# The last two feed-forwards of a four-layer kernel: up projections as seven block products, down projections spread between them

## The chip, the cores and the metric

The kernel runs on one core of a Trainium2 chip. The metric is the device time of one execution in microseconds, the median of several runs; lower is better. The profile is that of one more execution.

## The reference

A float32 transformer on 512 tokens of 1024 features: two blocks with convolutional feed-forwards, then two "hybrid" layers (differential attention, a gated recurrence, memory attention). What the change touches is the feed-forward of the two hybrid layers, here x is 512 x 1024, w_up 1024 x 5632, w_down 2816 x 1024:

```python
u = depthwise_conv_centred(x @ w_up, conv_w, conv_b)   # three taps over the tokens
gate, val = jnp.split(u, 2, axis=-1)
ffn = (jax.nn.silu(gate) * val) @ w_down
return layer_norm(DEEPNORM_ALPHA * x + ffn, ln2_g, ln2_b)
```

## The kernel before

Activations lie transposed, features on the partitions: X holds 8 tiles of 128 features x 512 tokens. A float32 product is made of three products of a shorter type: each operand is split in a high part and a low part (what the high part leaves), and PE adds high x high, high x low and low x high in one PSUM bank. HX holds both parts of the layer's input, FR those of the hidden activations.

**Weights.** They pass through a ring of SLOTS = 9 buffers of 128 x 1024. SyncE alone issues the loads, in one fixed order; the load of entry r waits until the user of entry r - 9 has freed it (L3516). A "unit" p is one weight tile. `cast_to` lets ScalarE (ACT) write its high part in WH[p % 3], after the load has landed and after PE has used unit p - 3; `rest_to` lets GpSimd (POOL) write the low part in WL[p % 3] and free the ring buffer (L452). Both take the units in order, and each engine runs its program in order, so a wait in it holds all that stands behind it. PE waits for the low part of each unit.

**Feed-forward before.** `ffn_plan` makes 44 up tiles (22 pairs of one gate and one val tile of 128 columns), 8 x 3 matmuls of 512 columns each. The hidden dimension is taken in two parts of 11 pairs; after each, 8 down groups (one for each output tile) run over its 11 hidden tiles, in two units of 6 and 5. For each up tile ACT makes the middle tap with the bias (L1051) and VectorE (DVE) the two outer taps from PSUM (L1055, L1058); then ACT makes silu (L1682), DVE gate x val (L1712), ACT the high part (L1688), DVE the low part (L1722). A down group is added to X by DVE (L2498, L2500); in the last part ACT squares X and POOL adds X and its square into the sums of the layer norm (L795).

**Start of a feed-forward.** The layer norm before it writes HX tile by tile (L896, L864). The first two up tiles run side by side behind it (`pair_pe`). `kept_a` (L904) then writes the normed X back, in the second layer with the casts of two units between. `mix_g` has left the low parts of units 0 to 2 ready.

## Time and profile before

| what | us |
|---|---|
| median of 3 runs (lowest, highest) | 3240.03 (3238.53, 3240.19) |
| span of the profiled execution | 3237.6 |
| PE busy | 3182.1 (98%) |
| first hybrid layer's feed-forward, up and down | about 2094 to 2446 |
| second one's | about 2874 to 3230 |

The span is the time from the first to the last instruction in the profile. The profile has no device time of its own execution; the span lies 2.4 us below the median of the runs. A matmul's duration in the profile holds its latency: the spacing of the starts says what one costs.

### The profile page before, as it was taken

The numbers are of one execution on the slowest core, as the hardware profiler recorded it, in microseconds if no ns is written. First come the engines' busy times: TensorE is split into PE (matmuls) and PEld (weight loads), VectorE is DVE, ScalarE is ACT, GpSimd is POOL, SyncE is SP. The second block draws the span as 40 slices with busy tenths as digits, with TensorE's granted clock in tenths as the row PEclk, the third lists the DMA queues.
The fourth block names the chain that finished last, engine by engine and source line by source line (L and its number), as shares of the span: only waits on it lengthen the run. The fifth ranks groups of instructions, "written<-read, shape, count | busy, mean of one in ns | idle before, by whom it ended". The sixth has DMA issues, their size and how long they took to land.

```text
span 3237.6 us, 40142 instructions
## 1 busy us (share of the span) xinstructions
PE 3182.1 (98%) x16204; PEld 2552.9 (79%) x16204; DVE 1591.0 (49%) x2605; ACT 1301.7 (40%) x2307; POOL 1329.3 (41%) x754
## 2 busy tenths in 40 slices
PE   7999999999999999999999999999999999999998
PEld 4876888888885557888886888888887788878886
DVE  5877366323337663423225685352432768455252
ACT  4322421312246774423334535342433544444243
POOL 2222423222254445444551234544455234454446
PEclk9999999999999999999999999999999999999999
DMA  7223334121132003233232111323223121222321
GB/s 274 105 96 121 124 110 147 49 66 66 52 115 103 20 8 116 93 93 105 82 117 72 54 59 53 117 93 101 96 90 114 46 70 45 62 98 76 116 79 55
DMA packets 85925, 288.17 MB, mean 89 GB/s; under 512 B 9803, under 2 KB 10379, under 8 KB 84972
## 3 DMA queue, kind: packets, MB, share of 16 engines
q1 hardware_dynamic: 85740, 285.60, 26.0%
q8 instruction: 128, 2.10, 0.3%
q14 instruction: 57, 0.47, 0.0%
HBM read 283.47 MB, written 2.10 MB: 88 GB/s over the span
## 4 chain that ended last, share of the span: by engine, by line
PE 89%; DVE 3%; issue 2%; POOL 2%; ACT 2%; DMA 1%; SPq 0%; POOLq 0%; DVEq 0%; ACTq 0%
PE ps L504 20%; PE ps L507 20%; PE ps L505 20%; PE ps L563 2%; PE ps L565 2%; PE ps L564 2%; PE ps L2153 2%; PE ps L3005 1%; PE ps L2596 1%; DMA ring<-in_w_mod 1%; PE ps L483 1%; PE ps L2223 1%; PE ps L478 1%; PE ps L522 1%; PE ps L2610 1%
## 5 line engine op out<-in xcount | busy, mean ns | idle before, releaser
L452 POOL TENSOR_TENSOR WL<-ring,WH 128x1024 fp32r<-128x1024 f32 (+2 forms) x427 | 926.6, 2173 | 1397.4 <-ACT WH L441 1397.0
L504 PE MATMUL ps<-HX,WH 128*128 128x512 f32 x1656 | 649.2, 392 | 0.0
L507 PE MATMUL ps<-HX,WL 128*128 128x512 f32 x1656 | 647.7, 391 | 0.0
L505 PE MATMUL ps<-HX,WH 128*128 128x512 f32 x1656 | 646.2, 390 | 0.0
L441 ACT CAST WH<-ring 128x1024 fp32r<-128x1024 f32 (+2 forms) x443 | 421.1, 951 | 529.5 <-PE ps L507 471.2
L504 PE MATMUL ps<-FR,WH 128*128 128x512 f32 x1120 | 418.8, 374 | 0.3
L505 PE MATMUL ps<-FR,WH 128*128 128x512 f32 x1120 | 409.7, 373 | 0.0
L507 PE MATMUL ps<-FR,WL 128*128 128x512 f32 x1120 | 389.4, 373 | 0.0
L504 PEld LDWEIGHTS ps<-HX,WH 128*128 128x128 f32 x1656 | 311.1, 188 | 67.2 <-issue 1.2
L507 PEld LDWEIGHTS ps<-HX,WL 128*128 128x128 f32 x1656 | 312.3, 189 | 45.0
L505 PEld LDWEIGHTS ps<-HX,WH 128*128 128x128 f32 x1656 | 311.3, 188 | 45.0
L1055 DVE SCALAR_TENSOR_TENSOR T<-ps,pv,T 128x511 f32<-128x511 f32 (+1 forms) x154 | 109.4, 711 | 346.5 <-ACT T L1051 342.3
L504 PEld LDWEIGHTS ps<-FR,WH 128*128 128x128 f32 x1120 | 210.3, 188 | 46.8 <-DVE FR L3218 1.1
L1051 ACT ACTIVATE T<-ps,pv 128x512 f32<-128x512 f32 (+1 forms) x154 | 112.7, 746 | 328.8 <-PE ps L507 317.3
L505 PEld LDWEIGHTS ps<-FR,WH 128*128 128x128 f32 x1120 | 210.4, 188 | 37.4
L507 PEld LDWEIGHTS ps<-FR,WL 128*128 128x128 f32 x1120 | 198.6, 189 | 29.9
L1010 DVE SCALAR_TENSOR_TENSOR X<-ps,mod,X 128x512 f32<-128x512 f32 x64 | 48.0, 751 | 301.1 <-PE ps L507 287.7
L1722 DVE TENSOR_TENSOR FR<-T,FR 128x512 fp32r<-128x512 f32 x110 | 138.8, 1277 | 62.7 <-ACT FR L1688 62.7
L505 PE MATMUL ps<-HC,WH 128*128 128x256 f32 x504 | 141.8, 281 | 0.0
L507 PE MATMUL ps<-HC,WL 128*128 128x256 f32 x504 | 141.5, 281 | 0.0
L504 PE MATMUL ps<-HC,WH 128*128 128x256 f32 x504 | 141.4, 281 | 0.0
L563 PE MATMUL ps<-WH,HX 128*128 128x512 f32 x320 | 126.8, 396 | 0.8 <-ACT AR L2694 0.8
(406 smaller groups left out, 5271.8 us busy)
## 6 DMA issues: line engine op xcount, KB each, us to landing
ring<-in_ffn_w_up SPq DMA_DIRECT2D x88, 512.0 KB, 3.2
ring<-in_w_up SPq DMA_DIRECT2D x88, 512.0 KB, 3.2
ring<-in_w_mod SPq DMA_DIRECT2D x64, 512.0 KB, 4.2
ring<-in_w_in_tok SPq DMA_DIRECT2D x40, 512.0 KB, 3.3
ring<-in_w_mod_columns SPq DMA_DIRECT2D x32, 512.0 KB, 4.1
ring<-in_w_in_feat SPq DMA_DIRECT2D x32, 512.0 KB, 3.2
ring<-in_ffn_w_down SPq DMA_DIRECT2D x32, 384.0 KB, 3.0
ring<-in_w_out SPq DMA_DIRECT2D x32, 384.0 KB, 3.1
```

The source lines that it names most:

```text
L441: act.copy(WH[:, p % SPLITS, 0:n], ring.ap(r)).then_inc(*split.a.up("high", p))
L452: pool.tensor_tensor(WL[:, p % SPLITS, 0:n], ring.ap(r), WH[:, p % SPLITS, 0:n], ALU.subtract).then_inc(*ring.frees(r, split.g, "low", p))
L504: pe.matmul(o, high, xh, first, False)
L505: pe.matmul(o, high, xl, False, False)
L507: m = pe.matmul(PS[bs[i]][:, 0:N], low, get(k)[0], False, last)
L563: pe.matmul(PS[bs[t]][:, :], xh[:, tt], high, k == 0, False)
L564: pe.matmul(PS[bs[t]][:, :], xh[:, tt], low, False, False)
L565: m = pe.matmul(PS[bs[t]][:, :], xl[:, tt], high, False, k == 7)
L1051: act.activation(dst, src, ACT.Identity, scale=w1, bias=b).then_inc(*steps.up("conv", *name))
L1055: dve.scalar_tensor_tensor(dst[:, 1:N], src[:, 0:N - 1], w0, dst[:, 1:N], ALU.mult, ALU.add).then_inc(*steps.up())
L1722: dve.tensor_tensor(lo, gate_tile(L, n, s, val_conv), hi, ALU.subtract).then_inc(*fw.v.up("low", L.name, n, s))
L2153: pe.matmul(PS[b][:, 0:c1 - c0], QT[n % 2][0:96, h, t * 128:t * 128 + 128], KT[n % 2][0:96, h, c0:c1], True, True).then_inc(*att.pe.up("sc ...
```

## The change

The two hybrid feed-forwards (L_ffb) get a plan and four engine programs of their own. Pairs 0 and 1 run as before. For the other 20 pairs the weights of a pair and the input are cut in 2 x 2 blocks (gate and val by the two halves of the 1024 features; tokens by halves of 256), and seven block products of 4 x 3 matmuls of 256 columns take the place of eight. The sums of weight blocks are made by DVE in the ring's buffers and in T, in float32; the sums of input blocks ("forms", XF) once for each layer, by DVE, then split by ACT and POOL. The products are summed in PSUM: each of them accumulates in a half of a bank, and copies by ACT (copy 1, 2, 3, 5) and two additions by DVE ("five right", "five both") put them where they are wanted. A pair takes four units: "11" (512 wide) in step i = j, "1 2" (1024) in the same step, "3 12" and "4 22" (1024 each) in step i = j + 1. The low part of "1 2" is made by DVE, the others by POOL. The hidden dimension is taken in parts of 3, 4, 5, 5 and 5 pairs, so that there are 40 down groups of one unit each; 28 of them stand one or two at a time behind the steps 4 to 21, one in step 22, 11 at the end. The ring has 8 buffers instead of 9, in the whole kernel.

```diff
-SLOTS = 9
+SLOTS = 8
-ARENA = 27200
+ARENA = 28224
+FRONT = 2
...
         HC = nc.alloc_sbuf_tensor_at("HC", [128, 8, 2, SC], F32R, offset=base + 4 * 20480)
+        XF = [nc.alloc_sbuf_tensor_at(f"XF{k}", [128, 2, 4, 256], F32R, offset=base + 4 * o)
...
+        def seven_plan(name, wname, dname, i):
+
+            L = Linear(ring, name)
+            L.sizes, L.nst, L.i, L.slots = [3, 4, 5, 5, 5], 1, i, 10
+            L.bounds = [sum(L.sizes[:p]) for p in range(len(L.sizes) + 1)]
+            up, down = dr[wname][i], dr[dname][i]
+            L.rows(up, 0, 2 * FRONT, 8, kind="up")
+            L.unit, L.downs, L.down_last = {}, {}, []
+            def made(kind, j, n, loads=()):
+                p = L.unit[kind, j] = len(ring.splits)
+                ring.splits.append((None, n))
+                ring.made[p] = (L, kind, j)
+                if loads:
+                    ring.carried[p] = [((L.name, x), up[x]) for j_ in loads for x in (2 * j_, 2 * j_ + 1)]
+
+            rows = [(x, n) for x in range(len(L.sizes)) for n in range(8)]
+
+            def some(at, n):
+                for _ in range(n):
+                    x, row = rows.pop(0)
+                    L.rows(down, row, row + 1, L.sizes[x], per=6, k0=L.bounds[x], kind=x)
+                    L.downs.setdefault(at, []).append(L.groups[-1])
+                    if row == 7:
+                        L.down_last.append(L.groups[-1].last)
+
+            after = dict(zip(range(4, 22), (2, 2, 2, 2, 2, 2, 2, 1, 1, 2, 2, 2, 1, 1, 1, 1, 1, 1)))
+            for j in range(FRONT, FT + 1):
+                if j < FT:
+                    made("11", j, 512, range(j, min(j + 2, FT)) if j == FRONT else range(j + 1, min(j + 2, FT)))
+                if j > FRONT:
+                    made("3 12", j - 1, 1024)
+                if j < FT:
+                    made("1 2", j, 1024)
+                else:
+                    some("between", 1)
+                if j > FRONT:
+                    made("4 22", j - 1, 1024)
+                some(j, after.get(j, 0))
+            some("end", len(rows))
             return L
...
+        in_vector |= {p for p, (_, kind, _) in ring.made.items() if kind == "1 2"}
+        def unit_source(p):
+
+            if p not in ring.made:
+                r = ring.place.get(p, 0)
+                return ring.ap(r), ring.landed(r)
+            L, kind, j = ring.made[p]
+            gate, val = raw_tiles(L, j)
+            if kind == "11":
+                return ring.ap(gate)[:, 0:512], ring.landed(gate)
+            if kind == "3 12":
+                return ring.ap(gate), sv.v.at("sum 3", L.name, j)
+            if kind == "1 2":
+                return T[:, 4:6, :].rearrange("p a b -> p (a b)"), sv.v.at("sum 2", L.name, j)
+            return ring.ap(val), sv.v.at("sum 4", L.name, j)
+
+        def low_up(steps, p):
+
+            if p not in ring.made:
+                return ring.frees(ring.place.get(p, 0), steps, "low", p)
+            up = steps.up("low", p)
+            L, kind, j = ring.made[p]
+            if kind == "4 22":
+                for r in raw_tiles(L, j):
+                    ring.frees_too(r, steps)
+            return up
...
         def cast_to(act, upto):
             while ring.cast <= min(upto, len(ring.splits) - 1):
                 p = ring.cast
                 ring.cast += 1
                 n = ring.splits[p][1]
-                r = ring.place.get(p, 0)
-                act.wait_ge(*ring.landed(r))
+                src, ready = unit_source(p)
+                act.wait_ge(*ready)
                 if p >= SPLITS:
                     act.wait_ge(*split.pe.at("used", p - SPLITS))
-                act.copy(WH[:, p % SPLITS, 0:n], ring.ap(r)).then_inc(*split.a.up("high", p))
+                act.copy(WH[:, p % SPLITS, 0:n], src).then_inc(*split.a.up("high", p))
...
+        def forms_v(dve, q):
+            for k in range(4):
+                dve.wait_ge(*nm.a.at("kept", q.name, k + 4))
+                b12, b21, b22 = BLOCKS[:, 2 * k + 1, :], BLOCKS[:, 2 * k + 8, :], BLOCKS[:, 2 * k + 9, :]
+                dve.tensor_tensor(raw_form(k, F1, 2).rearrange("p (a b) -> p a b", a=2), BLOCKS[:, 2 * k:2 * k + 10:9, :],
+                                  b12.unsqueeze(1).to_broadcast([128, 2, 256]), ALU.subtract).then_inc(*sv.v.up())
+                dve.wait_ge(*sv.v.now())
+                dve.scalar_tensor_tensor(raw_form(k, F2S), raw_form(k, F1), -1.0, b22, ALU.mult,
+                                         ALU.subtract).then_inc(*sv.v.up())
+                dve.wait_ge(*sv.v.now())
+                dve.scalar_tensor_tensor(raw_form(k, F4), raw_form(k, F2S), -1.0, b21, ALU.mult,
+                                         ALU.subtract).then_inc(*sv.v.up("forms", q.name, k))
+
+        def forms_a(act, q):
+            for k in range(4):
+                act.wait_ge(*sv.v.at("forms", q.name, k))
+                act.copy(XF[k][:, 0, :, :].rearrange("p a b -> p (a b)"), raw_form(k, 0, 4)).then_inc(
+                    *sv.a.up("forms", q.name, k))
+
+        def forms_g(pool, q):
+            for k in range(4):
+                pool.wait_ge(*sv.a.at("forms", q.name, k))
+                pool.tensor_tensor(XF[k][:, 1, :, :].rearrange("p a b -> p (a b)"), raw_form(k, 0, 4),
+                                   XF[k][:, 0, :, :].rearrange("p a b -> p (a b)"), ALU.subtract).then_inc(
+                    *sv.g.up("forms", q.name, k))
+
...
+        def product_pe(pe, p, at, out, x, ready=None, opens=None):
+
+            for k in range(4):
+                c = slice(at + k * 128, at + k * 128 + 128)
+                high, low = WH[:, p % SPLITS, c], WL[:, p % SPLITS, c]
+                xh, xl = x(k)
+                if ready is not None:
+                    for done in ready(k):
+                        pe.wait_ge(*done)
+                if k == 0 and opens == "whole bank":
+                    pe.matmul(out[0], high, HX[:, 0, 0, :], True, False)
+                else:
+                    pe.matmul(out[1], high, xh, k == 0 and opens == "half", False)
+                pe.matmul(out[1], high, xl, False, False)
+                m = pe.matmul(out[1], low, xh, False, k == 3)
+            return m
+
...
+            for i in range(FRONT, FT + 1):
+                j = i - 1
+                if i < FT:
+                    A[i], B[i] = bank.take_in("gate", "gate", name, i), bank.take_in("val", "val", name, i)
+                    C[i] = bank.take_in("five", "five", name, i)
+                    p = begin("11", i)
+                    if i < FRONT + 2:
+                        pe.wait_ge(*bank.free("val", name, i))
+                        pe.matmul(PS[B[i]][:, :], WH[:, p % SPLITS, 0:128], HX[:, 0, 0, :], True, True)
+                    pe.wait_ge(*bank.free("gate", name, i))
+                    product_pe(pe, p, 0, left(A[i]), block_of(0, 0), None, "whole bank").then_inc(*split.pe.up("used", p))
+                if j >= FRONT:
+                    p = begin("3 12", j)
+                    pe.wait_ge(*sv.a.at("copy 2", name, j))
+                    product_pe(pe, p, 0, right(B[j]), form_of(F3), formed).then_inc(*sv.pe.up("product 7", name, j))
+                    pe.wait_ge(*sv.v.at("five right", name, j))
+                    product_pe(pe, p, 512, left(A[j]), block_of(1, 0)).then_inc(*split.pe.up("used", p))
+                if i < FT:
+                    p = begin("1 2", i)
+                    pe.wait_ge(*bank.free("five", name, i))
+                    product_pe(pe, p, 0, left(C[i]), form_of(F1), formed, "half").then_inc(
+                        *sv.pe.up("product 5", name, i))
+                    pe.wait_ge(*sv.a.at("copy 1", name, i))
+                    product_pe(pe, p, 512, right(B[i]), form_of(F2S), formed).then_inc(*split.pe.up("used", p))
+                else:
+                    for g in L.downs["between"]:
+                        down(g)
+                if j >= FRONT:
+                    p = begin("4 22", j)
+                    product_pe(pe, p, 0, right(A[j]), block_of(1, 1)).then_inc(*sv.pe.up("product 3", name, j))
+                    pe.wait_ge(*sv.v.at("five both", name, j))
+                    product_pe(pe, p, 512, left(B[j]), form_of(F4), formed).then_inc(*split.pe.up("used", p))
+                for g in L.downs.get(i, ()):
+                    down(g)
+            for g in L.downs["end"]:
+                down(g)
+
...
+            forms_a(act, qf)
+            for g in [g for g in L.groups if g.key[0] == "up"]:
...
+            for i in range(FRONT, FT + 1):
+                j = i - 1
+                if FRONT < i < FT:
+                    cast_to(act, L.unit["11", i] + 3)
+                high(i - 2)
+                if i == FRONT:
+                    cast_to(act, L.unit["11", i] + 3)
+                if i < FT:
+                    act.wait_ge(*used("11", i))
+                    if i >= FRONT + 2:
+                        act.wait_ge(*bank.free("val", name, i))
+                    act.copy(val_bank(L, i)[:, 256:512], gate_bank(L, i)[:, 0:256]).then_inc(*sv.a.up("copy 1", name, i))
+                if j >= FRONT:
+                    act.wait_ge(*sv.pe.at("product 7", name, j))
+                    act.copy(val_bank(L, j)[:, 0:256], val_bank(L, j)[:, 256:512]).then_inc(*sv.a.up("copy 3", name, j))
+                    cast_to(act, L.unit["3 12", j] + 3)
+                if i < FT:
+                    act.wait_ge(*sv.pe.at("product 5", name, i))
+                    if i >= FRONT + 2:
+                        act.wait_ge(*sv.v.at("five both", name, i - 2))
+                    act.copy(five(i), ps("five", name, i)[:, 0:256]).then_inc(
+                        *bank.emptied(("five", name, i), sv.a, "copy 5", name, i))
+                    act.wait_ge(*used("1 2", i))
+                    act.copy(gate_bank(L, i)[:, 256:512], val_bank(L, i)[:, 256:512]).then_inc(
+                        *sv.a.up("copy 2", name, i))
+                    cast_to(act, L.unit["1 2", i] + 3)
...
+                if j >= FRONT:
+                    act.wait_ge(*sv.pe.at("product 3", name, j))
+                    act.wait_ge(*fw.v.at("low", name, j - 2, 0))
+                    conv_a(act, fw.a, (name, 2 * j, 0), T[:, j % 2, :], gate_bank(L, j)[:, :], cw(1, j), cb(j))
+                    cast_to(act, L.unit["4 22", j] + 3)
+                    act.wait_ge(*used("4 22", j))
+                    act.wait_ge(*sv.v.at("five both", name, j))
+                    conv_a(act, fw.a, (name, 2 * j + 1, 0), T[:, 2 + j % 2, :], val_bank(L, j)[:, :], cw(1, FT + j),
+                           cb(FT + j))
+                    act.wait_ge(*fw.v.at("conv", name, 2 * j, 0))
+                    act.activation(gate_bank(L, j)[:, :], T[:, j % 2, :], ACT.Silu).then_inc(
+                        *fw.a.up("silu", name, j, 0))
+                for g in L.downs.get(i, ()):
+                    down(g)
...
+            def sums_1_2(j):
+                gate, val = raw_tiles(L, j)
+                dve.wait_ge(*ring.landed(val))
+                dve.tensor_tensor(T[:, 4, :], ring.ap(val)[:, 0:512], ring.ap(val)[:, 512:1024], ALU.add).then_inc(
+                    *sv.v.up("sum 1", name, j))
+                dve.wait_ge(*ring.landed(gate))
+                dve.wait_ge(*sv.v.at("sum 1", name, j))
+                dve.tensor_tensor(T[:, 5, :], T[:, 4, :], ring.ap(gate)[:, 0:512], ALU.add).then_inc(
+                    *sv.v.up("sum 2", name, j))
+
+            def sums_3_4(j):
+                gate, val = raw_tiles(L, j)
+                dve.wait_ge(*low_done(L.unit["11", j]))
+                dve.tensor_tensor(ring.ap(gate)[:, 0:512], ring.ap(gate)[:, 0:512], ring.ap(val)[:, 0:512],
+                                  ALU.add).then_inc(*sv.v.up("sum 3", name, j))
+                dve.wait_ge(*sv.v.at("sum 3", name, j))
+                dve.tensor_tensor(ring.ap(val)[:, 0:512], T[:, 5, :], ring.ap(gate)[:, 512:1024],
+                                  ALU.add).then_inc(*sv.v.up("sum 4", name, j))
+
+            sums_1_2(FRONT)
+            forms_v(dve, qf)
...
+            for i in range(FRONT, FT + 1):
+                j = i - 1
+                if i < FT:
+                    rest_v(dve, L.unit["1 2", i])
+                low(i - 2)
+                if j >= FRONT:
+                    dve.wait_ge(*sv.a.at("copy 3", name, j))
+                    dve.wait_ge(*sv.a.at("copy 5", name, j))
+                    dve.tensor_tensor(val_bank(L, j)[:, 256:512], val_bank(L, j)[:, 256:512], five(j), ALU.add).then_inc(
+                        *sv.v.up("five both", name, j))
+                if i < FT:
+                    sums_3_4(i)
+                if i + 1 < FT:
+                    sums_1_2(i + 1)
+                if i < FT:
+                    dve.wait_ge(*sv.a.at("copy 2", name, i))
+                    dve.wait_ge(*sv.a.at("copy 5", name, i))
+                    dve.tensor_tensor(gate_bank(L, i)[:, 256:512], gate_bank(L, i)[:, 256:512], five(i),
+                                      ALU.add).then_inc(*sv.v.up("five right", name, i))
...
+                if j >= FRONT:
+                    taps(j, 0, gate_bank(L, j), None, T[:, j % 2, :])
+                    taps(j, 1, val_bank(L, j), ("val", name, j), T[:, 2 + j % 2, :])
+                    dve.wait_ge(*fw.v.now())
+                    dve.wait_ge(*fw.a.at("silu", name, j, 0))
+                    dve.scalar_tensor_tensor(gate_bank(L, j)[:, :], T[:, 2 + j % 2, :], -1.0, gate_bank(L, j)[:, :],
+                                             ALU.mult, ALU.mult).then_inc(*fw.v.up("gated", name, j, 0))
+                for g in L.downs.get(i, ()):
+                    down_v(dve, L, g)
+            low(FT - 1)
+            for g in L.downs["end"]:
+                down_v(dve, L, g)
+
+        def seven_g(pool, L, qf, q):
+            forms_g(pool, qf)
+            for g in L.downs["end"]:
+                rest_to(pool, g.last + 2)
+                if is_final(L, g):
+                    ln_sums_g(pool, q, g.key[1], lin.v.at("res", L.name, g.key, 0))
+            ln_g(pool, q)
+            rest_to(pool, g.last + 3)
...
-            ffn_v(dve, L_ffb[l], lambda j, n: col("conv_w_2", 132 * l + 44 * j + n), True, down)
+            seven_v(dve, L_ffb[l], lambda j, n: col("conv_w_2", 132 * l + 44 * j + n), ln_1[l], down)
...
-            last_ffn_a(act, L_ffb[l], ln_2[l], lambda j, n: col("conv_w_2", 132 * l + 44 * j + n),
-                       lambda n: col("conv_b_2", 44 * l + n), True)
+            seven_a(act, L_ffb[l], lambda j, n: col("conv_w_2", 132 * l + 44 * j + n),
+                    lambda n: col("conv_b_2", 44 * l + n), ln_1[l], ln_2[l])
...
-                ffn_pe(pe, L_ffb[l], lambda s: ready1)
+                seven_pe(pe, L_ffb[l], ln_1[l], ready1)
...
-                last_ffn_g(pool, L_ffb[l], ln_2[l])
+                seven_g(pool, L_ffb[l], ln_1[l], ln_2[l])
```

## Rows read from the trace of the kernel before

**Rows 1.** The page: span, PE's busy line, chain by engine.

```profile
span 3237.6 us, 40142 instructions
...
PE 89%; DVE 3%; issue 2%; POOL 2%; ACT 2%; DMA 1%; SPq 0%; POOLq 0%; DVEq 0%; ACTq 0%
```

**Rows 2.** Windows: window, length, busy us and count of PE, PEld, DVE, ACT, POOL; clock, DMA, GB/s.

```profile
2094.00:2446.00 352.00, 352.00 (x1578) 290.77 (x1577) 141.41 (x150) 133.72 (x175) 173.81 (x89) 1.00 0.30 97
2873.68:3230.00 356.32, 352.41 (x1581) 290.60 (x1579) 144.74 (x158) 137.59 (x184) 173.48 (x91) 1.00 0.25 80
```

**Rows 3.** Timeline of PE: start, duration; first matmuls of two neighbouring up tiles.

```profile
2873.68 0.39 PE L504 MATMUL ps<-HX,WH 128*128 128x512 f32 x1
...
2879.11 0.39 PE L504 MATMUL ps<-HX,WH 128*128 128x512 f32 x1
```

**Rows 4.** Timeline of PE in the first feed-forward: wide and narrow matmuls mixed.

```profile
599.95 0.39 PE L504 MATMUL ps<-HX,WH 128*128 128x512 f32 x1
...
602.51 0.28 PE L504 MATMUL ps<-HC,WH 128*128 128x256 f32 x1
602.63 0.28 PE L505 MATMUL ps<-HC,WH 128*128 128x256 f32 x1
602.75 0.40 PE L507 MATMUL ps<-HX,WL 128*128 128x512 f32 x1
...
611.53 0.40 PE L504 MATMUL ps<-HX,WH 128*128 128x512 f32 x1
```

**Rows 5.** Groups by form, 2094 to 2446, POOL: splitting a unit, layer-norm sums.

```profile
L452 POOL TENSOR_TENSOR WL<-ring,WH 128x1024 fp32r<-128x1024 f32 x43 | 103.2, 2401 | 128.5 <-ACT WH L441 128.5
L452 POOL TENSOR_TENSOR WL<-ring,WH 128x640 fp32r<-128x640 f32 x16 | 25.1, 1566 | 24.5 <-ACT WH L441 24.5
L795 POOL TENSOR_TENSOR T<-T,X 128x512 f32<-128x512 f32 x6 | 7.7, 1286 | 9.8 <-DVE X L2500 9.8
```

**Rows 6.** Timeline, start of the first hybrid feed-forward.

```profile
2087.91 5.03 ACT L904 ACTIVATE X<-X,pv 128x512 f32<-128x512 f32 x8
...
2095.14 0.39 PE L504 MATMUL ps<-HX,WH 128*128 128x512 f32 x1
```

**Rows 7.** Timeline of ACT, start of the second one.

```profile
2876.22 2.56 ACT L904 ACTIVATE X<-X,pv 128x512 f32<-128x512 f32 x4
```

**Rows 8.** Timeline of DVE and POOL: one DVE form beside a POOL operation, and alone.

```profile
2101.04 2.36 DVE L1712 TENSOR_TENSOR T<-T 128x512 f32<-128x512 f32 x1
...
2100.45 2.40 POOL L452 TENSOR_TENSOR WL<-ring,WH 128x1024 fp32r<-128x1024 f32 x1 [1.15 <-ACT WH L441]
...
2883.95 0.69 DVE L1712 TENSOR_TENSOR T<-T 128x512 f32<-128x512 f32 x1
```

**Rows 9.** Groups by form of the whole span: DVE subtraction of 1024, taps.

```profile
L1058 DVE SCALAR_TENSOR_TENSOR T<-ps,pv,T 128x511 f32<-128x511 f32 x132 | 99.0, 750 | 4.7
...
L429 DVE TENSOR_TENSOR WL<-ring,WH 128x1024 fp32r<-128x1024 f32 x12 | 16.5, 1377 | 1.6 <-ACT WH L441 1.6
```

**Rows 10.** Groups by form of the whole span, ACT: casts, middle tap, narrow copy.

```profile
L441 ACT CAST WH<-ring 128x1024 fp32r<-128x1024 f32 x283 | 295.3, 1044 | 238.1 <-PE ps L507 179.8 <-PE ps L565 58.1 <-PE ps L483 0.2
L1051 ACT ACTIVATE T<-ps,pv 128x512 f32<-128x512 f32 x132 | 102.7, 778 | 328.8 <-PE ps L507 317.3 <-PE ps L483 10.0
L441 ACT CAST WH<-ring 128x640 fp32r<-128x640 f32 x64 | 46.4, 725 | 141.3 <-PE ps L507 141.3
...
L2207 ACT COPY AR<-ps 128x256 f32<-128x256 f32 x32 | 12.2, 381 | 0.0
```

**Rows 11.** DMA issues (KB each, us to landing), and windows of full DMA load.

```profile
ring<-in_w_up SPq DMA_DIRECT2D x88, 512.0 KB, 3.2
...
ring<-in_w_down SPq DMA_DIRECT2D x32, 320.0 KB, 2.8
...
10.00:16.00 6.00, 0.00 (x0) 0.00 (x0) 1.26 (x3) 2.42 (x5) 0.00 (x0) 1.00 1.00 410
```

**Rows 12.** Timeline of POOL in the last down groups.

```profile
3174.61 1.57 POOL L452 TENSOR_TENSOR WL<-ring,WH 128x640 fp32r<-128x640 f32 x1 [0.93 <-ACT WH L441]
3177.92 1.29 POOL L795 TENSOR_TENSOR T<-T,X 128x512 f32<-128x512 f32 x1 [1.74 <-DVE X L2500]
3179.17 1.29 POOL L795 TENSOR_TENSOR T<-T 128x512 f32<-128x512 f32 x1
3180.42 3.38 POOL L452 TENSOR_TENSOR WL<-ring,WH 128x768 fp32r<-128x768 f32 x2
3185.40 1.28 POOL L795 TENSOR_TENSOR T<-T,X 128x512 f32<-128x512 f32 x1 [1.61 <-DVE X L2500]
```

More of the change, by code:

```diff
@@ L219, in ask @@
             src, n = self.splits[self.asked]
-            self.place[self.asked] = self.raw(src, n)
+            for key, tile in self.carried.get(self.asked, ()):
+                self.named[key] = self.raw(tile, SLOT)
+            if src is not None:
+                self.place[self.asked] = self.raw(src, n)
             self.asked += 1
@@ L426, in rest_v @@
         def rest_v(dve, p):
[L427 removed]
+            n = ring.splits[p][1]
             dve.wait_ge(*split.a.at("high", p))
[L429 to L430 removed]
+            dve.tensor_tensor(WL[:, p % SPLITS, 0:n], unit_source(p)[0], WH[:, p % SPLITS, 0:n],
+                              ALU.subtract).then_inc(*low_up(split.v, p))
         def cast_to(act, upto):
@@ L3260, in ffb_v @@
+        def seven_g(pool, L, qf, q):
+            forms_g(pool, qf)
+            for g in L.downs["end"]:
+                rest_to(pool, g.last + 2)
+                if is_final(L, g):
+                    ln_sums_g(pool, q, g.key[1], lin.v.at("res", L.name, g.key, 0))
+            ln_g(pool, q)
+            rest_to(pool, g.last + 3)
         def ffb_v(dve, l, kept):
```

130 lines of the change are left out of this document (120 added, 10 removed).

## The prediction

> **What bounds the kernel now.** I read the page first: PE is busy for nearly the whole span and the chain that ended last is PE's for 89% [rows 1]. Then the windows of the two stages that change: in both PE has no idle time to speak of, DVE and ACT are busy about 40% and POOL about half, TensorE at full clock (2.4 GHz) [rows 2]. So a microsecond taken from PE's stream is a microsecond of the kernel, and one in which PE waits there is one lost. The question is what a narrow matmul costs, and which engine in front of PE becomes late.
>
> **PE's stream, the gain.** An up tile of 24 wide matmuls takes 2879.11 - 2873.68 = 5.43 us, 0.226 us each [rows 3]; a pair (48) 10.86. The new pair has 84 matmuls of 256 columns, one of them opened over the whole bank (512). Their price is not shown in a pure stream. In the first feed-forward, where two wide and two narrow alternate, a narrow one is followed after 0.12 us [rows 4]. Over the whole stretch of 11 rounds, 33 wide and 33 narrow in 611.53 - 599.95 = 11.58 us, what 33 wide ones leave is 0.125 for a narrow one; the lower bound is half a wide one, 0.113. I take 0.12, the direct spacing: 84 x 0.12 + 0.11 for the wide opening = 10.19, a gain of 0.67 a pair, 27 us over 2 x 20 pairs. At 0.125 it is 11 us, at 0.113 it is 49.
>
> The Trainium skill ("TensorE: Matmul & The Clock Gate", Back-to-back issue gap) gives an isolated gap of columns / 2.4 + 2.5 ns, 109 ns for 256 columns, and warns that the load of the weights is not in it. By its figure the gain would be an estimated 64 us; no run here shows so short a spacing, and the sum doesn't use it.
>
> The down matmuls stay the same in number (528 a layer) and width: nothing on PE.
>
> **Start of each layer, a loss.** `forms_g` is the first thing in POOL's program, and the low part of unit 3 (up tile 3) stands behind it; `mix_g` has made units 0 to 2 only. The four forms are each of the size of a unit: POOL 2.40 [rows 5], ACT 1.04 [rows 10]. ACT copies the first when `kept_a` is done. First layer: 2087.91 + 5.03 = 2092.94 [rows 6], ACT to 2094.0, POOL 4 x 2.4 to 2103.6, unit 3 to 2106.1. PE wants it after up tile 2, 2095.14 + 5.43 = 2100.6: 5.5 us late. Second layer: kept done at 2878.8 [rows 7], less 0.4 for the narrower cast between, POOL from 2879.5 to 2889.1, unit 3 at 2891.5, wanted at 2873.68 + 5.43 = 2879.1: 12.4 late. Together 18 us at least. It grows because DVE's form operations read two SBUF operands: such an operation took 2.36 us beside a POOL operation and 0.69 without [rows 8]. The third and fourth form have three of these each, and with one POOL operation to be sat out by several of them the two layers lose some 9 us more: between 18 and 27, I take 22.
>
> Behind it, DVE must finish both taps and the product of pair 1 before `rest_v` of the first "1 2": ACT 0.78, two taps 2 x 0.79, product 0.69, subtraction 1.4 [rows 9, 10] = 4.5 us after up tile 3, of which unit "11" (12 x 0.12 + 0.11 = 1.55) covers a third. PE waits 3 us a layer, 6 in all. In step 3, which has no down group, the same chain is late again by 1 to 3 us: 3 in all.
>
> **Every step, the large loss.** Put t = 0 where PE ends "11" of pair i. PE then has "3 12", "1 2", "4 22", 24 narrow matmuls or 2.88 each, and reaches the first down unit D at 8.64. The cast of "4 22" (pair i - 1) must wait for t = 0, because it takes the WH buffer of "11"; ACT 1.04, POOL 2.40 and the hand-overs put its low part at 3.6. Only this frees both raw tiles of pair i - 1. The order of the ring in step i is gate and val of pair i + 1, then the down tiles. With two down tiles in each of the two steps before, entry r - 8 of the next gate tile is the gate tile of pair i - 1: SyncE issues it at 3.6, val, and then D behind them, although D's own buffer is long free. A load alone took 3.2 us for 512 KB, and under full load the chip moved 410 GB/s [rows 11]: 1.28 us of data, 1.9 fixed. Gate, val and D (197, 262 or 328 KB for 3, 4, 5 tiles) are 3.0 to 3.4 us of data, so D lands at 8.5 to 8.9, where PE would already use it. ACT's cast takes 0.5 to 0.73 and POOL 1.0 to 1.57 (the rows at 640 and 1024 set the line) [rows 5, 10]: low part at 10.2, 10.8 or 11.4, PE late by 1.6, 2.2 or 2.8 us. So it is in steps 6 and 7 (size 3), 8 to 11 (size 4), 15 and 16 (size 5): 17.6. In steps 12, 14 and 17 three down tiles stand in the two steps before: gate comes early, val and D are issued at 3.6, D late by 0.9 to 1.4: 3.7. In 5, 13 and 18 to 21 only D is behind, 2.8 us to land [rows 11], late by 0.2: 1. Together 22 a layer, 44 in all. While ACT stands in the cast of D, copies 5 and 2, the cast of the next down unit and the middle taps are queued behind it; DVE waits for those and for val's landing in `sums_1_2`. They would end in time for the next step, save that the cast of "3 12" comes about 1 us late behind the short downs of size 3. Bounds: 12 if each load landed in its lone time (D at 7.1), 52 with this second delay.
>
> The other work has cover. DVE has for a pair four sums of 512, the subtraction, two narrow additions, four taps, the product and the low part, some 9.5 us [rows 8, 9], and a step of PE takes 13 to 17 with its downs; the locks of rows 8 add up to 3. ACT has 3.7 us of casts, four copies of 0.38, two taps, silu and high part, about 8. POOL has 6.1 and 1.0 to 1.57 for each down unit.
>
> **The end.** The last 8 down groups take PE 15 x 0.226 = 3.4 us each instead of 7.5, but POOL still has for each the unit of 1.57 and two sums of 1.29, with gaps 4.3 us [rows 12]. Before, there was an idle 1.6 in each period of 7.5. POOL falls behind by 0.9 a group after a slack of about two units; in the first layer the splits of the next stage (2.4 each) come in too. The layer norm starts later by 2 us in the second and 3.5 in the first layer: 5.5, between 2 and 10.
>
> **The ring of 8.** Elsewhere SyncE mostly waits for buffers whose entries are long unused; where loads are late a buffer less costs one load's spacing. I take 2, between 0 and 8.
>
> **The sum.** -27 (PE) + 22 (forms) + 6 + 3 (first steps) + 44 (loads and splits of the downs) + 5.5 (end) + 2 (ring) = +55.5. The profiled span of 3237.6 [rows 1] becomes 3293; with the 2.4 us around it to the median, 3295.
>
> **Rivals.**
> *The loads of the downs come in time.* If ACT finds D landed by 7, or PE's steps are longer than I think, the 44 go to 0 or little. For it speaks that no PE wait on a load is seen in these stages today; against it that the raw tiles are now held for a step and a half. The rest then is 38.5 against the gain: +11.5, 3251. This is the case on the other side: it is not slower (3246 or below) where the narrow matmul costs 0.1185 us or less, within rows 4's spread, and it would be faster from 0.115. Chance 0.17, of which 0.06 the same and 0.02 faster.
> *The narrow stream runs at half the wide spacing*, 0.113: gain 49 instead of 27, 3273. The page's figure cited above points the same way. Rows 4 speak against it. Chance 0.1.
> *DVE and POOL stand in each other's way.* Five operations of a pair have two SBUF operands, and each can sit out a POOL operation of up to 2.4 us. If 0.5 to 1 us of that reaches PE in each of 40 pairs, 20 to 40 more: 3315 to 3335. DVE's spare time speaks against it. Chance 0.15.
> *Forecast as summed*: 0.55. Left for a gain that I don't see: 0.03.
>
> **Range and chances.** All terms at their low ends (gain 49, then 18, 4, 12, 2, 0) give 3227, all at their high ends (gain 11, then 27, 12, 52, 10, 8) 3338. Two in ten are left out: 3242 to 3328. Forecast, narrow stream and engine rival are slower, and half of the first rival (0.09). A change within 0.2% (6.5 us) is about what a measurement of this kernel can't tell from none. Faster 0.05, the same 0.06, slower 0.89.
>
> **What would show it.** In the profile after: PE's busy spacing of narrow matmuls 0.12; a wait of PE for POOL's low part of 5 to 18 us at up tile 3 of each layer, right behind `forms_g`; in steps 6 to 11 a PE wait of about 2 us before the first down group, with ACT's cast released by a load; PE waits for POOL in the last down groups. The prediction is wrong if PE's waits in the steps are absent (then 3250), or if narrow matmuls start every 0.11 us or less.

## The result, and the profile after

The changed kernel takes 3385.12 us (median of 4, 3383.06 to 3387.58), the kernel before 3239.65 (median of 4, 3238.53 to 3240.19): a ratio of 1.0447 [1.0432, 1.0462], 145 us slower. The prediction had the sign and 55.5 us; the time lies outside its range.

The page of the changed kernel answers to [rows 1] and [rows 11]; in its fifth part the columns are busy us, mean ns, and the idle time ahead with its releaser:

```profile
span 3385.1 us, 43945 instructions
...
PE 77%; POOL 6%; DMA 5%; DVE 5%; ACT 4%; issue 3%; SPq 1%; POOLq 0%; DVEq 0%; ACTq 0%
...
L583 PE MATMUL ps<-FR,WH 128*128 128x512 f32 x1120 | 431.4, 385 | 60.7 <-POOL WL L531 60.4
L583 PE MATMUL ps<-HX,WH 128*128 128x512 f32 x1016 | 402.0, 396 | 22.2 <-POOL WL L531 22.2
...
L3390 PE MATMUL ps<-XF,WH 128*128 128x256 f32 x640 | 184.3, 288 | 16.1 <-DVE WL L509 13.5
...
ring<-in_w_up SPq DMA_DIRECT2D x88, 512.0 KB, 4.3
...
ring<-in_w_down SPq DMA_DIRECT2D x48, 320.0 KB, 3.9
```

The span grew by 147.5 us and PE's share of the chain fell from 89% to 77%; POOL's rose from 2% to 6%, DMA's from 1% to 5%, ACT's from 2% to 4%. Three lines name new waits of PE: 60.4 us ahead of down matmuls (`FR`), 22.2 ahead of an up tile (`HX`), 16.1 in the seven-product pairs (`L3390`). They come to 99, so something else took the rest.

PE's waits in the changed kernel (total us, times, longest):

```profile
PE ps L583 <- POOL WL L531: 82.6, 32, 14.5
PE ps L671 <- DMA ring<-in_w_mod: 32.3, 11, 16.5
...
PE ps L1537 <- DMA ring<-in_idft: 2.3, 1, 2.3
```

`w_mod` and `idft` belong to stages whose code the change does not touch. Before, the `w_mod` wait was 19.6 us, of which 16.0 is the wait for the first load at the start of the kernel; that one is 16.5 here.

Windows of PE in the changed kernel (window, length, busy us and count, granted clock, DMA share, GB/s), the first two for [rows 2]:

```profile
2123.26:2502.00 378.74, 335.05 (x2183) 0.96 0.24 82
2954.40:3384.00 429.60, 364.04 (x2303) 0.93 0.21 73
...
2135.00:2140.00 5.00, 3.40 (x8) 0.50 0.34 105
...
3050.00:3052.00 2.00, 2.00 (x6) 0.50 0.00 0
...
3241.00:3244.00 3.00, 2.86 (x7) 0.50 0.00 0
3244.00:3247.00 3.00, 3.00 (x9) 0.50 0.00 0
...
3227.69:3247.50 19.81, 16.70 (x100) 0.83 0.28 97
2399.28:2416.34 17.06, 13.92 (x101) 1.00 0.32 113
```

A clock of 0.50 is the 1.2 GHz level. The place of the loss can be read from the start of the first hybrid feed-forward, 2095.14 before [rows 6] and 2123.26 now, and of the second, 2873.68 [rows 3] and 2954.40:

| stretch | us more |
|---|---|
| ahead of the first hybrid feed-forward | 28.1 |
| from there to the start of the second | 52.6 |
| from there to the end | 66.8 |

### The profile page after: what moved, and what is told of

Read it like the earlier page. It is cut to its first block, busy times and chain, and to the rows that moved or that the text cites. A ratio compares the mean times of both kernels' runs of the same rounds, so it can differ in the third digit from the quotient of the medians.

```text
span 3385.1 us, 43945 instructions
## 1 busy us (share of the span) xinstructions
PE 3214.5 (95%) x17648; PEld 2632.6 (78%) x17648; DVE 1811.5 (54%) x2959; ACT 1413.3 (42%) x2571; POOL 1405.5 (42%) x818
## 4 chain that ended last, share of the span: by engine, by line
PE 77%; POOL 6%; DMA 5%; DVE 5%; ACT 4%; issue 3%; SPq 1%; POOLq 0%; DVEq 0%; ACTq 0%
PE ps L583 16%; PE ps L586 15%; PE ps L584 15%; POOL WL L531 4%; DMA ring<-in_w_down 4%; PE ps L642 2%; PE ps L643 2%; PE ps L644 2%; ACT WH L521 2%; PE ps L2232 1%; PE ps L3084 1%; DMA ring<-in_w_mod 1%; PE ps L3392 1%; PE ps L3391 1%; PE ps L1450 1%
## 5 line engine op out<-in xcount | busy, mean ns | idle before, releaser
L531 POOL TENSOR_TENSOR WL<-ring,WH 128x1024 fp32r<-128x1024 f32 (+4 forms) x483 | 983.4, 2043 | 1442.7 <-ACT WH L521 1442.5
L521 ACT CAST WH<-ring 128x1024 fp32r<-128x1024 f32 (+4 forms) x499 | 449.4, 901 | 690.2 <-PE ps L586 399.3
L583 PE MATMUL ps<-FR,WH 128*128 128x512 f32 x1120 | 431.4, 385 | 60.7 <-POOL WL L531 60.4
L583 PE MATMUL ps<-HX,WH 128*128 128x512 f32 x1016 | 402.0, 396 | 22.2 <-POOL WL L531 22.2
L584 PE MATMUL ps<-FR,WH 128*128 128x512 f32 x1120 | 418.4, 381 | 0.0
L586 PE MATMUL ps<-HX,WL 128*128 128x512 f32 x1016 | 399.7, 393 | 0.0
L584 PE MATMUL ps<-HX,WH 128*128 128x512 f32 x1016 | 398.4, 392 | 0.0
L583 PEld LDWEIGHTS ps<-FR,WH 128*128 128x128 f32 x1120 | 215.1, 192 | 115.0 <-POOL WL L531 67.4
L584 PEld LDWEIGHTS ps<-FR,WH 128*128 128x128 f32 x1120 | 215.5, 192 | 38.0
L583 PEld LDWEIGHTS ps<-HX,WH 128*128 128x128 f32 x1016 | 191.8, 189 | 66.1 <-POOL WL L531 23.1
L586 PEld LDWEIGHTS ps<-HX,WL 128*128 128x128 f32 x1016 | 193.0, 190 | 20.5
L584 PEld LDWEIGHTS ps<-HX,WH 128*128 128x128 f32 x1016 | 192.0, 189 | 19.9
L3390 PE MATMUL ps<-XF,WH 128*128 128x256 f32 x640 | 184.3, 288 | 16.1 <-DVE WL L509 13.5
L3391 PE MATMUL ps<-XF,WH 128*128 128x256 f32 x640 | 182.8, 286 | 0.0
L3392 PE MATMUL ps<-XF,WL 128*128 128x256 f32 x640 | 182.6, 285 | 0.0
```

The costliest lines, as they stand in the source:

```text
L521: act.copy(WH[:, p % SPLITS, 0:n], src).then_inc(*split.a.up("high", p))
L531: pool.tensor_tensor(WL[:, p % SPLITS, 0:n], unit_source(p)[0], WH[:, p % SPLITS, 0:n], ALU.subtract).then_inc(*low_up(split.g, p))
L583: pe.matmul(o, high, xh, first, False)
L584: pe.matmul(o, high, xl, False, False)
L586: m = pe.matmul(PS[bs[i]][:, 0:N], low, get(k)[0], False, last)
L3390: pe.matmul(out[1], high, xh, k == 0 and opens == "half", False)
```

## The experiments

Twelve kernels in four groups; each group shares its own runs of the kernel before, and the ratio is taken to those. No kernel leaves work out.

| kernel | us | ratio to before |
|---|---|---|
| before, ring of 8 | 3268.59 | 1.0082 [1.0065, 1.0099] |
| after, ring of 9 | 3304.89 | 1.0198 [1.0183, 1.0214] |
| after, down loads ahead | 3310.75 | 1.0216 [1.0201, 1.0232] |
| after, unit 3 ahead of the forms | 3380.91 | 1.0429 [1.0414, 1.0445] |
| f1: ring of 9 and down loads ahead | 3274.02 | 1.0101 [1.0086, 1.0117] |
| f2: f1, units 3 and 4 ahead of the forms | 3259.39 | 1.0058 [1.0043, 1.0073] |
| f3: f2, "1 2" low parts of pairs 2 to 4 on POOL | 3252.76 | 1.0039 [1.0026, 1.0051] |
| f4: f3, first "1 2" between the forms, two casts later | 3257.98 | 1.0053 [1.0040, 1.0065] |
| f5: f4 with four plain pairs in front | 3248.47 | 1.0024 [1.0015, 1.0033] |
| f6: f5 with those low parts on DVE | 3252.43 | 1.0035 [1.0022, 1.0047] |
| f7: f5, one cast earlier | 3245.52 | 1.0014 [1.0005, 1.0023] |
| f8: f7, the end on POOL reordered | 3242.62 | 1.0010 [1.0002, 1.0019] |

### The kernel before with the ring of the changed one

```diff
-SLOTS = 9
+SLOTS = 8
```

> The kernel before with a ring of 8 buffers instead of 9, nothing else. In the changed kernel everything ahead of the first hybrid feed-forward is 28.1 us later, though the change does not touch that code. Theory (the ring): one buffer less makes the late loads of w_mod and of the following weights later; the same 28 us appear here, so 3240 + 25 to 30 = 3265 to 3270, with the PE waits on in_w_mod rising from 19.6 to about 32 us. Rival (my prediction's 2 us; the 28 come from somewhere else in the new program): 3240 to 3248.

Measured: 3268.59 us against 3241.18, 27.4 more, as the theory had it. Its waits, and two windows of PE in stages far from the change:

```profile
PE ps L592 <- DMA ring<-in_w_mod: 33.7, 10, 16.9
...
PE ps L1458 <- DMA ring<-in_idft: 3.6, 1, 3.6
```

```profile
300.00:380.00 80.00, 75.49 (x466) 0.98 0.23 76
1240.00:1320.00 80.00, 74.97 (x373) 0.91 0.32 119
```

In the kernel before, the same two windows have PE busy 79.84 and 79.93 us at clock 1.00. The start of the kernel hides where the waits are new. From 40 us on, the kernel before (first line) has one wait for a `w_mod` load, the one with eight buffers (second line) five:

```profile
PE ps L592 <- DMA ring<-in_w_mod: 1.1, 1, 1.1
PE ps L592 <- DMA ring<-in_w_mod: 14.3, 5, 4.5
```

The waits for loads grow by 14 (`w_mod`) and 3.6 (`idft`, where 1.6 us of another wait go), the span by 31; of the rest, 14 us are more busy time of PE for the same matmuls (3196.3 against 3182.1), beside a lower clock, as the second window shows. The third up tile of the first hybrid feed-forward starts at 2126.15 instead of 2095.14 [rows 6]: 31.0 us of the profiled execution's 31.1 lie ahead of it. So a buffer of the ring is worth 27 us in this kernel, with no word of the feed-forward changed, and it accounts for the 28.1 ahead of it in the changed kernel.

### The changed kernel with nine buffers, and with its down loads earlier

```diff
-SLOTS = 8
+SLOTS = 9
-ARENA = 28224
+ARENA = 27648
```

> The changed kernel with 9 ring buffers (the arena trimmed to what is used, 27648). Theory (the ring): the 28 us ahead of the hybrid layers vanish; in the steps with two downs in each of the two steps before, only the val tile now waits for the low part of '4 22', so the first down's load is issued behind one tile instead of two and its wait falls from 2 to 3 us to 1 to 1.5, all waits before downs from 60 to about 30 us, and the half-clock time behind them with it: 3385 - 28 - 30 - 10 to 15 = 3312 to 3317. Rival (waits before downs are a matter of the POOL and ACT chain alone): only the 28 us go, 3357.

Measured: 3304.89 us, 80 less than the changed kernel and 7 below the theory's 3312; the rival's 3357 is excluded. `w_mod` is back at 19.5 us, PE's wait at the forms of the first layer begins at 2100.19 instead of 2128.86, so the loss ahead of that layer is gone, and the waits ahead of the downs fall from 60.4 to 24.7 (the 46.9 of the row less the 22.2 of the forms):

```profile
PE ps L583 <- POOL WL L531: 46.9, 22, 14.5
PE ps L671 <- DMA ring<-in_w_mod: 19.5, 6, 16.7
```

The other way to get the downs in time: keep eight buffers, but let the raw tiles of the next pair be taken a step later, so that the down tiles stand ahead of them in the ring.

```diff
-made("11", j, 512, range(j, min(j + 2, FT)) if j == FRONT else range(j + 1, min(j + 2, FT)))
+made("11", j, 512, range(j, j + 1))
```

> The changed kernel, but the raw tiles of a pair stand in the ring's order behind the down tiles of the step before instead of ahead of them (a pair's tiles are asked for with its own unit '11'). Theory (the queue order): the down tile is loaded long before ACT casts it, the PE waits before the first down of each step (60 us in all) fall below 10, and the low clock behind them goes too, some 20 us: 3385 - 50 - 20 = 3300 to 3320. Rival (transfers too slow, or POOL and ACT too late whatever the order): waits stay above 40, 3365 or more. A second rival: DVE now waits longer for the pair's tiles in its sums and hands the wait to '1 2': the waits move to DVE's low parts, 3340 to 3385.

Measured: 3310.75 us, 74 less. No wait is left ahead of any down group, and new small ones, 1.8 us at most, stand at "3 12":

```profile
PE ps L583 <- POOL WL L531: 22.2, 2, 14.5
...
PE ps L3390 <- POOL WL L531: 9.6, 9, 1.8
```

The waits that went are 60.4 less 9.6 = 51 us, the time that came back is 74. A microsecond of wait costs nearly one and a half here.

### One unit ahead of the forms

```diff
 def seven_g(pool, L, qf, q):
+    rest_to(pool, [g for g in L.groups if g.key[0] == "up"][-1].last)
     forms_g(pool, qf)
```

(and the same on ACT with `cast_to`.)

> The changed kernel, with the cast and the low part of up tile 3 ahead of the forms on ACT and POOL. Theory: the PE waits of 7.7 and 14.5 us at up tile 3 vanish; since the forms then end 2.4 us later, PE waits in part for the last form at the first '1 2', 0 to 2 in the first and 4 to 6 us in the second layer, and the low clock behind the long wait goes in part: 3385 - 22 + 5 - 3 = 3362 to 3370. Rival (the forms themselves are the limit and only the place of the wait moves): 3380 to 3385.

Measured: 3380.91 us, 4 less, within the rival's range: my theory missed. The 22.2 us at the up tile are gone, 12.6 of them are back one unit later (`L3434` waits for "11" of the first pair):

```profile
PE ps L3434 <- POOL WL L531: 12.6, 2, 8.6
```

What counts is that POOL has four forms (4 x 2.4 us) to make among units that PE needs every 5 us or less. Moving one unit moves the place of the wait. Some 10 us of wait went in all, but PE's busy time grew from 3214.5 to 3220.9 for the same matmuls, so only 4 came back: the price of a wait is not the same in each edit.

### Both ring edits, then the start of the layer

f1 joins the nine buffers and the earlier down loads.

> The changed kernel with 9 ring buffers and the down tiles' loads ahead of the next pair's (the two earlier edits together). Theory (two separate causes, the ring ahead of the hybrid layers and the queue order in the steps): 28 us less than with the order alone, and the small waits on '3 12' that were left there gone: 3310.8 - 28 - 10 = 3270 to 3282. Left are the waits at up tile 3 (22 us), at the first '1 2' units (13.5) and the half clock behind them (about 10), against the 27 that PE gains. Rival (both cure the same wait): 3295 or more.

3274.02 us. This is within the theory's range. With 3304.89 and 3310.75 for each alone, the earlier loads are worth 31 on nine buffers and 74 on eight, 111 together where the sum of both alone is 154: the loss ahead of the layers is the ring's alone, but the lateness of the downs, which the order cures, is cured in part by the ninth buffer too.

f2 takes units 3 and 4 ahead of the forms:

```diff
+rest_to(pool, L.unit["11", FRONT])
 forms_g(pool, qf)
```

(and the same on ACT with `cast_to`.)

> As f1, and the casts and low parts of both up tile 3 and the first unit '11' ahead of the forms on ACT and POOL (the earlier edit moved only up tile 3 and its wait went to that unit '11'). Theory: the waits of 7.7 and 14.5 us go; the forms end later, and PE waits for them or for the low part of the first '1 2' by 3 to 6 us a layer; the low clock of these waits goes too: f1 - 15 to 22, 3250 to 3262. Rival (the forms are needed so early that the wait only moves once more): within 5 us of f1.

3259.39 us, 15 less. The wait moves on, now to the first "1 2":

```profile
PE ps L3390 <- DVE WL L509: 29.8, 4, 15.4
```

It is not the forms that PE waits for there. In the second layer POOL ends the last one at 2897.69, but ACT casts "1 2" behind the forms and the first taps (2898.39), and DVE, which has the taps and products of the plain pairs in front of it, makes the low part only here:

```profile
2905.22 1.21 DVE L509 TENSOR_TENSOR WL<-T,WH 128x1024 fp32r<-128x1024 f32 x1
```

f3 gives the low parts of "1 2" of pairs 2, 3 and 4 to POOL:

```diff
+def p_late(m):
+    return m[2] >= FRONT + 3
...
-in_vector |= {p for p, (_, kind, _) in ring.made.items() if kind == "1 2"}
+in_vector |= {p for p, (_, kind, _) in ring.made.items() if kind == "1 2" and p_late(ring.made[p])}
...
```

> As f2, with the low parts of the '1 2' units of pairs 2, 3 and 4 made by POOL instead of DVE. Theory (DVE is late in the steps without downs: its chain of taps, product and four sums ends after PE wants '1 2'): the waits of 4.1 us in step 4 and the half clock behind them go, 8 + 5 us in both layers, part of the 2.6 in step 2 too: f2 - 8 to 16. Rival (the sums themselves, not the subtraction, are late: unit '1 2' of pair 4 is cast only when sum 2 is made): f2 within 4 us.

3252.76 us, 6.6 less, a little short of the 8 to 16 expected: the wait of 4.0 us in step 4 is gone in both layers, but 21.7 us of wait for POOL remain, the longest 11.3, at the first "1 2". f4 puts the cast and the low part of that unit between the second and the third form. It has a second edit: the casts that stand between the writing back of X (`kept_a`) come three tiles later.

```diff
-if 3 <= j < 3 + casts:
+if 6 <= j < 6 + casts:
     cast_to(act, ring.cast)
...
 for k in range(4):
+    if k == 2:
+        rest_to(pool, L.unit["1 2", FRONT])
```

> As f3, with the two casts that interrupt the writing back of X in the second layer moved three tiles later, and the cast and low part of the first '1 2' unit placed between the second and the third form on ACT and POOL. In f3 PE waits 4.6 us in the first and 11.3 us in the second layer at the first '1 2', and runs at half clock behind it: 9 and 18 us lost. Theory (that unit's cast stands behind the forms and the first taps): most of this goes, f3 - 8 to 15, 3238 to 3245. Rival (the forms themselves, slowed by DVE and POOL blocking each other, are what PE waits for): f3 - 0 to 5.

3257.98 us, 5 more than f3: this theory fell. Which of the two edits costs the 5 us was not tried apart. The waits of the changed start are mostly for ACT's copies and for nothing that the profile shows ("issue"):

```profile
PE ps L3397 <- issue: 10.9, 2, 9.9
PE ps L3397 <- ACT ps L3524: 10.4, 2, 5.5
PE ps L3397 <- POOL WL L534: 6.1, 10, 1.0
```

### More plain pairs to cover the forms

f5 leaves four plain pairs in front instead of two and puts a unit ahead of the third and of the fourth form (f4's later casts stay in f5 to f8); 18 of 22 pairs are then of seven products.

```diff
-FRONT = 2
+FRONT = 4
...
```

> As f4, but the first four pairs of a layer run as plain products (18 by seven products), so that the forms are wanted 22 us later. Theory (the only loss left of size is the start of each layer, 28 us of waits and half clock in f3): it goes, at the price of the gain of two pairs a layer (2.7 us): 3252.8 - 28 + 2.7 = 3226 to 3232, below the kernel before. Rival (the start's lateness comes from the first block-product steps themselves, the chain of copies and sums, wherever they stand): 3240 to 3250.

3248.47 us, far from the 3226 to 3232 expected and within the rival's 3240 to 3250. PE still waits 10.8 us for a plain up tile and 6.9 for "1 2" units. f6 is f5 with all low parts of "1 2" back on DVE.

> As f5, with all '1 2' low parts on DVE as in the changed kernel. From pair 4 on each step has its downs, so DVE has time: if DVE was late only for want of downs in the steps, this is within 3 us of f5, or below it because POOL is relieved; if DVE's chain is late in the first steps in any case, it is 5 to 12 us above f5.

3252.43 us, 4 more, between the two cases that were expected, and the intervals of f5 and f6 overlap: the engine that makes these low parts matters little here, and which is better isn't shown. f7 is f5 with one cast (unit 7) ahead of the taps of pair 1:

```diff
+if n == 1 and not val:
+    cast_to(act, g.last + 5)
```

> As f5, with the cast of the last plain up tile (unit 7) placed on ACT ahead of the first taps of pair 1. In f5 PE waits for its low part, 3.6 us in the first and 7.0 us in the second layer, since ACT is behind with the taps that had to wait for the forms. Theory: these waits and the low clock behind them go, 8 to 13 us: 3235 to 3241. Rival (ACT's and DVE's backlog only shows up at the next unit): within 4 us of f5.

f8 is f7 with POOL adding the last but one tile to the layer-norm sums before it splits a unit of the next stage:

```diff
 for g in L.downs["end"]:
-    rest_to(pool, g.last + 2)
+    if g.key[1] != 6 or not is_final(L, g):
+        rest_to(pool, g.last + 2)
```

> As f7, with POOL adding output tile 6 to the layer-norm sums before it splits the first unit of the next stage (the rest of the order kept). PE waits 2.45 us for these sums at the end of the first hybrid layer. Theory: that wait goes, f7 - 2 to 3. Rival: the split is then late and PE waits for it after the layer norm: f7 - 1 to + 2.

3245.52 us for f7: 3 less than f5 where 8 to 13 were expected, so its rival held. The 10.8 us at the plain tile are gone, 3.0 and some 5 more stand at later units. 3242.62 us for f8: the 3 less that were expected, and the wait of 2.4 us for the layer-norm sums is gone. f8 is the best version, 0.1% behind the kernel before, and does not beat it. Its waits, and a window in the middle of the first hybrid feed-forward:

```profile
PE ps L3397 <- POOL WL L534: 13.1, 8, 3.3
...
PE ps L3441 <- POOL WL L534: 3.0, 1, 3.0
```

```profile
2134.00:2384.00 250.00, 246.74 (x1726) 0.99 0.28 97
```

By the measured rates 18 pairs in two layers gain 24 us. The waits of its two starts take 16 back. Some 10 more are not accounted for one by one. There is low clock in two opening steps (0.87 and 0.88); the refill behind each wait and the end of each layer are candidates. That stays open.

## Why the prediction was right and wrong

**The narrow matmul, right.** Step 3 of the changed kernel has no wait and takes 10.18 us from one "11" to the next: 83 x 0.12 + 0.23. In the kernel with the down loads ahead, each step without a wait takes 13.61 us with one size-5 down group or 17.01 with two, so the downs cost what they did. The gain of 27 us is there (0.67 x 40, from the price of a step). The rival "narrow stream at 0.113" and the spacing of 109 ns are excluded.

**The forms, right.** The wait stands behind up tile 2 of each layer, released by POOL's low part, 7.74 and 14.49 us: 22.2 against 22. Without the lock of DVE and POOL the prediction had 5.5 and 12.4, so each layer lost some 2 us more, in line with the gap of 1.91 us below. Timeline of the changed kernel, first layer (start, us, engine):

```profile
2122.09 5.36 POOL L3368 TENSOR_TENSOR XF<-AR,XF 128x1024 fp32r<-128x1024 f32 x2 [12.93 <-ACT XF L3362]
...
2122.31 2.89 DVE L3350 TENSOR_TENSOR AR<-X 128x512 f32<-128x512 f32 x1
...
2125.24 2.50 DVE L3353 SCALAR_TENSOR_TENSOR AR<-AR,X 128x256 f32<-128x256 f32 x1
...
2128.11 0.69 DVE L3350 TENSOR_TENSOR AR<-X 128x512 f32<-128x512 f32 x1
...
2128.83 0.42 DVE L3353 SCALAR_TENSOR_TENSOR AR<-AR,X 128x256 f32<-128x256 f32 x1
...
2129.36 4.88 POOL L3368 TENSOR_TENSOR XF<-AR,XF 128x1024 fp32r<-128x1024 f32 x2 [1.91 <-ACT XF L3362]
...
2136.60 0.79 PE L583 MATMUL ps<-HX,WH 128*128 128x512 f32 x1 [7.74 <-POOL WL L531]
```

POOL has a gap of 1.91 us between the second and the third form, in which it waits for ACT's copy and so for DVE's operations of 2.89 and 2.50 us. Alone they take 0.69 and 0.42. This is what [rows 8] showed. The Trainium skill ("SBUF — State Buffer", SBUF: two separate sides) says of a VectorE operation with two SBUF inputs and a GpSimd operation that reads SBUF that the one which starts first has the shared port for its whole length and the other is blocked; the trace agrees, with 2.89 against 0.69 and 2.50 against 0.42.

**The first steps, mis-sized.** 15.2 us (each layer 2.64 and 0.87 in step 2, 4.12 in step 4) of wait against 9; the late low part from DVE is as described, but it returns in step 4, not 3.

**The downs, mechanism right, size off.** The chain of waits repeats as I had it, here in step 6 of the second layer (PE ends "11" at 3038.16):

```profile
3038.18 1.06 ACT WH L521
...
3039.31 2.42 POOL WL L531
...
3041.75 0.33 SPq L3912
...
3042.12 0.43 SPq L3912
...
3042.59 4.49 DMA ring<-in_w_down
...
3047.70 1.25 POOL WL L531
```

The low part of "4 22" ends at t + 3.6, as computed. Then SyncE issues gate, val and D some 0.4 us apart, which I had left out, and D lands at t + 8.9 instead of 8.5; its low part is there at t + 10.8 instead of 10.2. The waits by step, first and second layer:

| steps | predicted each | measured |
|---|---|---|
| 6, 7 | 1.6 | 2.00, 1.76; 1.84, 2.02 |
| 8 to 11 | 2.2 | 2.01, 2.39, 2.61, 3.73; 3.61, 4.19, 2.42, 2.57 |
| 12, 14 | 0.9 to 1.4 | 1.17, 1.65; 1.48, 2.83 |
| 15, 16 | 2.8 | 2.95, 2.95; 4.25, 3.11 |
| 17 | 0.9 to 1.4 | 3.14; 1.83 |
| 13, 18 to 20 | 0.2 | 0.27 to 0.54; 0.34 to 1.12 |

60.4 us against 44. The size by size pattern is that of the sum, some steps a microsecond or more longer. In the first layer's chain the load of D takes 4.55 us from issue to landing in step 9 and 4.72 in step 15. In steps 8, 9 and 15 of the second layer, the long ones, it takes

```profile
3078.83 5.19 DMA ring<-in_w_down
...
3099.37 6.36 DMA ring<-in_w_down
...
3210.69 6.02 DMA ring<-in_w_down
```

and in step 8 SyncE's issue ahead of D takes 1.36 us instead of 0.43. So the extra time of these steps is mostly in the loads; why these land later stays open.

**The end, mis-sized.** PE shows 2.4 us of wait for POOL at the end of the first layer and none in the second, against 5.5.

**The ring of 8, a step that failed.** I wrote "elsewhere SyncE mostly waits for buffers whose entries are long unused" and "I take 2, between 0 and 8". The kernel before with eight buffers shows 27. Its new waits are for loads of `w_mod` and `idft` ahead of the hybrid layers, three of them of some 4 us (4.51 before 377.81, 3.97 before 952.26, 4.26 before 1305.47). At none of these places did the kernel before have a wait for a load: of its 19.6 us for `w_mod`, 16.0 stand at the start of the kernel and only 1.1 behind 40 us. So the profile of before gave no warning in its waits. What the missing buffer does is seen in the issues: before, the last `w_mod` load of the stage was issued at 363.03; with eight buffers it is issued at 374.26 and lands at 377.77, where PE waits for it. I had looked for late loads only in the stages that the change rewrites.

**The clock, the step that failed by most.** I wrote that a microsecond "in which PE waits there is one lost", and the sum took every PE wait at its own length, with nothing for what follows it. The windows above show what follows a wait. In step 16 of the second layer PE is idle from 3238.03 for 3.11 us, and the granted clock is 0.50 in 3241 to 3247. Timeline of PE, the first down matmuls there and in step 17 of the first layer, where a wait of 3.14 us left the clock at 1.00:

```profile
3241.14 0.80 PE L583 MATMUL ps<-FR,WH 128*128 128x512 f32 x1 [3.11 <-POOL WL L531]
...
3242.59 0.63 PE L583 MATMUL ps<-FR,WH 128*128 128x512 f32 x1
...
3243.87 0.63 PE L583 MATMUL ps<-FR,WH 128*128 128x512 f32 x1
...
2412.76 0.50 PE L583 MATMUL ps<-FR,WH 128*128 128x512 f32 x1 [3.14 <-POOL WL L531]
...
2413.58 0.40 PE L583 MATMUL ps<-FR,WH 128*128 128x512 f32 x1
...
2414.27 0.39 PE L583 MATMUL ps<-FR,WH 128*128 128x512 f32 x1
```

Three matmuls take 1.28 us in the one and 0.69 in the other. Without its wait the step takes 13.61; 13.61 + 3.11 = 16.72, and it took 19.81, 3.1 more. Step 17 took 17.06, 0.3 more than 13.61 + 3.14. So a wait cost 0.3 us beside itself where the clock stayed (I call this refill), and about 3 us in the one step where the clock fell behind it. In the first feed-forward stretch the sum is -13.5 (gain) + 45.8 (waits), and 52.6 was measured, which leaves 20 us. In the second it is -13.5 + 54.6 against 66.8, which leaves 26. These 46 us are what the sum leaves over, not a measured term; they are put down to refill and low clock because the granted clock over the two windows, (1 - 0.96) x 379 and (1 - 0.93) x 430, gives 15 and 30 at most, and because in the reordered kernel 51 us of wait took 23 us more with them when they went. Length alone does not decide it: behind a wait of 1.84 us, which ends at 3048.99, the clock was 0.50 too (3050 to 3052 above), behind that of 3.14 us it was 1.00. What decides these runs do not tell.

The sum with what was measured: 28.1 (ring) - 27 (gain) + 22.2 (forms) + 15.2 (first steps) + 60.4 (downs) + 2.4 (end, first layer) + 46 (what is left over) = 147. The ring's 28.1 hold low clock too. Against +55.5 this is 46 more for the clock and refill, 26 for the ring, 16 for the downs, 6 for the first steps, and 3 less for the end.

**The rivals.** *Loads of the downs in time* is excluded as a description of the change and realised by the reordered loads: even then, on nine buffers, f1 is 33 us slower than before where that rival had 11.5. *DVE and POOL in each other's way*: in the kernel with the down loads ahead, steps with downs of size 5 and no wait take their PE time (10.19 + 3.4 = 13.6), so beyond the start of each layer no such loss is seen.

## What to carry to other kernels

A profile in which PE is never idle says that the loads are in time with this depth of the ring and this order of entries, not that they have slack: here a buffer less cost 27 us in stages whose load waits had come to 1.1 us. Before a buffer is given up, follow each entry to the one whose buffer it takes, in every stage, or run the old kernel with the smaller ring. Price a wait of TensorE above itself in a kernel that otherwise runs at the full clock: 74 us came back for 51 us of wait, though a single edit gave 4 for 10. A cheaper product pays only when the operands' preparation has a cover at the start: the best arrangement here gained 24 us in the stream and gave them all back.

## What the runs showed of the hardware

- TensorE's granted clock was 0.50, the 1.2 GHz level, behind waits of 7.74 us (2135 to 2140), 3.11 us (3241 to 3247) and 1.84 us (3050 to 3052); behind one of 3.14 us it stayed at 1.00 (2399.28 to 2416.34).
- A DVE operation of two SBUF operands took 2.89 and 2.50 us beside POOL against 0.69 and 0.42 alone; the form with a scalar (SCALAR_TENSOR_TENSOR) is held just as the plain one.
- A load of a down tile (197 KB) took 4.49 us from issue to landing behind two of 512 KB, and one of 262 KB took 4.55 us in step 9 of the first layer and 6.36 in step 9 of the second; the issues on SyncE's queue mostly stood 0.4 us apart.
- Matmuls of 256 columns ran at an even 0.12 us with a new weight load each, over pairs of 84.
